# One hybrid attention, SSD and expert step on one Trainium2 core: SSD chunks moved in between the query and gate projections

## What is computed

```python
mod = jnp.dot(jax.nn.silu(cvec), lp['ada_w']) + lp['ada_b']        # 6 x 1024 columns
sh1, sc1, g1, sh2, sc2, g2 = jnp.split(mod[:, None, :], 6, axis=-1)
h = rmsnorm(x, lp['norm1']) * (1 + sc1) + sh1
proj = jnp.dot(h, lp['w_in'])                                      # 2064 columns
q, k, v, xbc, z, dt_raw = jnp.split(proj, SPLITS, axis=-1)
q = rmsnorm(q.reshape(b, L, N_HEADS, HEAD_DIM), lp['q_norm'])      # then rotated; k too
attn = block_attention(q, keys, vals)
xbc = jax.nn.silu(centred_dwconv(xbc, lp['conv_w'], lp['conv_b']))
ssm, h_fin = ssd_mixer(xbc, z, dt_raw, h0, ...)                    # chunks of 128, both directions, times silu(z)
x = x + g1 * jnp.dot(jnp.concatenate([attn, ssm], axis=-1), lp['w_out'])
h2 = rmsnorm(x, lp['norm2']) * (1 + sc2) + sh2
x = x + g2 * expert_choice_ffn(h2, ...)                            # 16 experts, SwiGLU
```

## Time and profile before

| | us |
|---|---|
| median of 3 runs | 2115.31 (2110.8 to 2117.49) |
| the profiled execution, its time | 2113.7 |
| its span, first to last instruction | 2112.0 |
| mean granted clock of TensorE, 1.0 being 2.4 GHz | 0.932 |
| PE busy | 1876.4 (89%) |
| DVE busy | 648.7 (31%) |
| ACT busy | 351.0 (17%) |
| POOL busy | 195.9 (9%) |

### The profile page before, as it was taken

The page is one execution under the profiler, slowest core; times in us unless marked ns, Lnnn a source line. Parts: engine busy times, 40 slices in busy tenths (PEclk is TensorE's granted clock), DMA queues, the critical chain, the costliest instruction groups (busy, mean ns, idle before and its releaser), DMA issues. The chain is left out here.

```text
span 2112.0 us, 34478 instructions
## 1 busy us (share of the span) xinstructions
PE 1876.4 (89%) x14896; PEld 909.8 (43%) x14896; DVE 648.7 (31%) x1360; ACT 351.0 (17%) x872; POOL 195.9 (9%) x265
## 2 busy tenths in 40 slices
PE   4999788984999999999839998789859999999997
PEld 1453664442344434444315536644413434444343
DVE  2314557334111212112123155673341112112121
ACT  2211533120100100001022115332101001000010
POOL 0002310000000001000010023100000001010010
PEclk9999769996999999999869997799979999999998
DMA  9632010332999999999953320103339999999993
GB/s 388 237 127 93 27 58 1 140 141 90 335 404 393 408 406 401 411 398 403 385 226 120 119 103 18 58 1 149 142 108 342 405 396 403 407 398 409 405 404 111
DMA packets 56870, 526.47 MB, mean 249 GB/s; under 512 B 11950, under 2 KB 13598, under 8 KB 26046
## 3 DMA queue, kind: packets, MB, share of 16 engines
q1 hardware_dynamic: 42062, 482.30, 56.5%
q0 software_dynamic: 6336, 21.63, 4.3%
q10 hardware_dynamic: 8416, 21.76, 2.7%
HBM read 503.91 MB, written 24.38 MB: 250 GB/s over the span
## 5 line engine op out<-in xcount | busy, mean ns | idle before, releaser
L503 PE MATMUL PS<-arena,xe 128*32 128x512 f32 x6144 | 673.4, 598 | 3.8 <-DVE xe L1212 3.8
L503 PEld LDWEIGHTS PS<-arena,xe 128*32 128x32 f32 x6144 | 195.9, 111 | 457.9 <-issue 453.6
L527 PE MATMUL PS<-arena,hdT 128*32 128x512 f32 x1536 | 269.0, 600 | 12.4 <-DMA arena<-w_exp 10.5
L529 PE MATMUL PS<-arena,hdT 128*32 128x256 f32 x1024 | 266.6, 383 | 0.0
L1223 DVE TENSOR_TENSOR RA<-RA,PS 96x512 f32<-96x512 f32 (+2 forms) x96 | 63.2, 684 | 648.8 <-ACT RA L948 646.1
L580 PE MATMUL PS<-arena,RB 128*128 128x512 f32 (+1 forms) x480 | 176.7, 528 | 0.0
L532 PE MATMUL PS<-arena,hdT 128*32 128x256 f32 x1536 | 157.3, 382 | 0.0
L533 PE MATMUL PS<-arena,hdT 128*32 128x256 f32 x512 | 153.6, 382 | 0.0
L853 PE MATMUL PS<-arena,RB 128*128 128x512 f32 x320 | 138.8, 593 | 2.0 <-DVE RB L1471 2.0
L948 ACT ACTIVATE RA<-PS 96x512 f32<-96x512 f32 x32 | 19.0, 593 | 689.4 <-PE PS L503 689.4
L580 PEld LDWEIGHTS PS<-arena,RB 128*128 128x128 f32 x480 | 90.4, 190 | 87.5 <-issue 81.3
(11 more groups left out here) (269 smaller groups left out, 1818.4 us busy)
## 6 DMA issues: line engine op xcount, KB each, us to landing
arena<-w_exp SPq DMA_DIRECT2D x192, 2048.0 KB, 12.3
arena<-ada_rest SPq DMA_DIRECT2D x16, 2048.0 KB, 7.6
arena<-w_in SPq DMA_DIRECT2D x4, 4128.0 KB, 31.3
ada<-ada_first SPq DMA_DIRECT2D x8, 2048.0 KB, 22.9
arena<-w_out SPq DMA_DIRECT2D x2, 4096.0 KB, 12.9
RC<-x_res ACTq DMA_DIRECT2D x2, 2560.0 KB, 9.8
x_res<-RC ACTq DMA_DIRECT2D x10, 512.0 KB, 2.6
normed_rows<-RA ACTq DMA_DIRECT2D x10, 512.0 KB, 2.6
```

The source lines that it names most:

```text
L503: last = mm(PS[GRP * q:GRP * (q + 1), c * 512:(c + 1) * 512], xe[:, k, GRP * grp:GRP * (grp + 1)], w[:, col_, :], start=(k == 0), stop=(k ...
L527: mm(PS[GRP * q:GRP * (q + 1), 1536:2048], tok(q), w[:, 0:512], start=first, **flags)
L529: mm(PS[96:P, 1536 + grp * REST:1536 + (grp + 1) * REST], tok(grp), w[:, MAIN:D], start=first and grp == 0, **flags)
```

## The change

- w_in is stored by groups of use: the six chunks of convolved columns (x0 and x1, three each), keys with step sizes (kv), queries (q) and z, each a transfer and a semaphore of its own. Layer 0 loads x0, x1, slabs 0 and 1, kv, q, the small loads, z, then the other slabs. Layer 1 loads x0, x1, kv and z, then waits for the rows of x and loads slabs 0 and 1 and q.
- A slab stands behind each chunk of the convolved columns (six), the last two behind key tiles 1 and 3.
- PSUM: the products use four banks up to number 16 and two from there on; the other banks serve the SSD pieces.
- `project` takes a `midway` that runs between its steps k = 3 and 4. The token transposes stand from key tile 3 to query tile 1, the sums behind query tile 1, the modulation rows amid query tile 2, `cumulated` and `scores` of chunks 0 and 1 and the state products around query tiles 2 to 4. Chunk t stands amid z tile t.
- Queries are squared, summed and rotated tile by tile inside DVE's loop over chunks (`head_sums`, `head_norms`), keys before the sums; the powers are split (`query_root`). The product with silu(z) moves from `tile_out` behind the rotation.
- Chunk buffers move into the part of the arena that the convolved columns' weights leave, temporaries into RA.

The core of the diff (indented 8 less; "..." for what is left out; removed lines only where they help):

```diff
-C_Q, C_KV, C_DT, C_XBC, C_Z = 0, 512, 768, 784, 1552
+KV_DT = 272
+W_Z, W_X, W_K, W_Q = 0, 4096, 10240, 12416
...
+EW = [a.rearrange("p (r c) -> p r c", r=2) for a in (arena[:, 8192:10240], arena[:, 10240:12288])]
...
+        def input_weights(group, a, n):
+            sp.dma_start(arena[:, a:a + n], row(w_in, l)[:, :, a:a + n].rearrange("a p n -> (a p) n")).then_inc(win_in[group].sem, 16)
+        def slab(c):
             if c >= 2:
...
+        if l:
+            sp.wait_ge(gu_used.sem, gu_used.at(l, 0))
+        input_weights("x0", W_X, 3072)
+        input_weights("x1", W_X + 3072, 3072)
+        if l:
+            input_weights("kv", W_K, KD * KV_DT)
+            input_weights("z", W_Z, KD * 512)
+            sp.wait_ge(x_in.sem, x_in.at(l, 2))
+            sp.wait_ge(dn_used.sem, dn_used.at(l, 0))
+            slab(0)
+            slab(1)
+            input_weights("q", W_Q, KD * 512)
+        else:
+            slab(0)
+            slab(1)
+            input_weights("kv", W_K, KD * KV_DT)
+            input_weights("q", W_Q, KD * 512)
+            sp.dma_start(ropes[:, :, :], rope).then_inc(rope_in, 16)
+            caches(0)
+            input_weights("z", W_Z, KD * 512)
+        for c in range(2, KD):
+            slab(c)
+        if l == 0:
+            sp.dma_start(x_res[0:CTX, :], x_prompt).then_inc(x_copied, 16)
...
+        def project(width, lhs, rhs, midway=None):
...
+        def states():
+            pe.wait_ge(tok_ev.sem, tok_ev.at(l, NT))
+            pe.wait_ge(mod_rdy2.sem, mod_rdy2.at(l, 1))
+            pe.wait_ge(gm_rdy.sem, gm_rdy.at(l, 1))
...
+            if t or r:
+                pe.wait_ge(c_rdy.sem, c_rdy.at(l, 2 * t + r))
+            else:
+                pe.wait_ge(cs_rdy.sem, cs_rdy.at(l, 1))
+                pe.wait_ge(hp_rdy.sem, hp_rdy.at(l, 1))
             for h in range(8):
...
+        for c in range(NC_):
+            if c == 0:
+                pe.wait_ge(win_in["x0"].sem, win_in["x0"].at(l, 1))
+            if c == 3:
+                pe.wait_ge(win_in["x1"].sem, win_in["x1"].at(l, 1))
+            for _, s0, sn in (SETS[1], SETS[0]):
+                project(sn, lambda k: arena[:, W_X + c * 1024 + k * P:W_X + c * 1024 + (k + 1) * P], lambda k: hT[:, k, s0:s0 + sn])
+            rest_of_modulation(c)
...
+        pe.wait_ge(win_in["kv"].sem, win_in["kv"].at(l, 1))
+        for t in range(NT):
+            project(KV_DT, tokens(t), lambda k: arena[:, W_K + k * KV_DT:W_K + (k + 1) * KV_DT])
+            if t == 1:
+                rest_of_modulation(6)
+            if t == 3:
+                rest_of_modulation(7)
+                conv_tokens(0)
+        conv_tokens(1)
+        def queries(t, midway):
+            project(512, tokens(t), lambda k: arena[:, W_Q + k * 512:W_Q + (k + 1) * 512], midway)
+        pe.wait_ge(win_in["q"].sem, win_in["q"].at(l, 1))
+        queries(0, lambda: conv_tokens(2))
+        conv_tokens(3)
+        queries(1, lambda: conv_tokens(4))
+        sums()
+        first_states()
+        queries(2, second_rows)
+        cumulated(0, 0)
+        scores(0)
+        queries(3, lambda: cumulated(0, 1))
+        states()
+        queries(4, lambda: cumulated(1, 0))
+        cumulated(1, 1)
+        scores(1)
+        pe.wait_ge(win_in["z"].sem, win_in["z"].at(l, 1))
+        for t in range(NT):
+            def chunk():
+                if t and t + 1 < NT:
+                    cumulated(t + 1, 1)
+                if t:
+                    from_states(t)
+                else:
+                    last_states()
+                within_chunk(t)
+                if t + 2 < NT:
+                    scores(t + 2)
+            project(512, tokens(t), lambda k: arena[:, W_Z + k * 512:W_Z + (k + 1) * 512], chunk)
             if t + 2 < NT:
-                scores(t + 2)
-                for r in range(2):
-                    cumulated(t + 2, r)
-            if t == 0:
-                pe.wait_ge(hf_ev.sem, hf_ev.at(l, 1))
+                cumulated(t + 2, 0)
         pe.wait_ge(y_done.sem, y_done.at(l, NT))
...
+        def clamped(t, r):
+            act.wait_ge(seg_ps.sem, seg_ps.at(l, 2 * t + r + 1))
+            if t >= 2:
+                act.wait_ge(yd_ps.sem, yd_ps.at(l, 2 * (t - 2) + r + 1))
+            for h in range(8):
+                o = 1024 + h * P
+                last = A(EW[t % 2][:, r, h * P:(h + 1) * P], PS[:, o:o + P], ACT.Relu, scale=-1.0, bias=cs[:, r, t, h:h + 1])
+            last.then_inc(c_rdy.sem, 1)
+        def decays(t):
+            for r in range(2):
+                act.wait_ge(c_rdy.sem, c_rdy.at(l, 2 * t + r + 1))
+                A(EW[t % 2][:, r, :], EW[t % 2][:, r, :], ACT.Exp, scale=-1.0).then_inc(e_rdy.sem, 1)
+        keys_evac(0)
+        keys_evac(1)
+        keys_evac(2)
         conv_silu(NC_ - 1)
...
+        keys_evac(3)
+        tokens_evac(0)
+        keys_evac(4)
         A(negA[:, :], bp[:, B_AL:B_AL + 16], ACT.Exp)
+        tokens_evac(1)
         act.wait_ge(dt_abs.sem, dt_abs.at(l, 1))
         A(dte[:, :, :], dts[:, :, :], ACT.Exp, scale=-1.0).then_inc(dt_e.sem, 1)
...
         act.wait_ge(rows0_2.sem, rows0_2.at(l, 1))
         act.wait_ge(ada2_used.sem, ada2_used.at(l, KD))
         for q in (0, 1):
             last = A(mrows2[32 * q:32 * q + 2, :, :], PS[32 * q:32 * q + 2, 3072:4096].rearrange("p (b c) -> p b c", b=2), ACT.Copy)
         last.then_inc(rows_act2.sem, 1)
...
+        tokens_evac(2)
+        queries_evac(0)
+        tokens_evac(3)
+        tokens_evac(4)
+        queries_evac(1)
+        act.wait_ge(cs_rdy.sem, cs_rdy.at(l, 1))
+        A(wend[:, :, :, :], wend[:, :, :, :], ACT.Exp)
+        A(ecs[:, :, :, :], cs[:, 0:2, :, :], ACT.Exp)
+        A(etot[:, :, :, :], cs[:, 2:4, :, :], ACT.Exp).then_inc(cs_e.sem, 1)
+        queries_evac(2)
+        clamped(0, 0)
+        clamped(0, 1)
+        decays(0)
+        queries_evac(3)
         act.wait_ge(S_ps.sem, S_ps.at(l, 4))
+        clamped(1, 0)
+        queries_evac(4)
+        clamped(1, 1)
+        decays(1)
         for t in range(NT):
...
             if t == 0:
                 act.wait_ge(hf_ps.sem, hf_ps.at(l, 1))
                 act.wait_ge(h0_ps.sem, h0_ps.at(l, 1))
                 A(hst[:, :, :, :].rearrange("p r m c -> p (r m c)"), bank(6), ACT.Copy).then_inc(hf_ev.sem, 1)
...
+            elif t + 1 < NT:
+                clamped(t + 1, 1)
+                decays(t + 1)
+            act.wait_ge(ip_ps.sem, ip_ps.at(l, n + 1))
+            A(z_t[:, t, :], bank(place(n)), ACT.Silu).then_inc(ip_ev.sem, 1)
+            n += 1
+            if t + 2 < NT:
+                clamped(t + 2, 0)
+            if t:
+                act.wait_ge(y_done.sem, y_done.at(l, t))
+                squares(l, 1, t - 1, cat[:, t - 1, 512:1024], sqtmp)
+        act.wait_ge(y_done.sem, y_done.at(l, NT))
+        squares(l, 1, NT - 1, cat[:, NT - 1, 512:1024], sqtmp)
         act.wait_ge(hf_ev.sem, hf_ev.at(l, 1))
         for r in range(2):
...
-        link(V.tensor_copy(cs[:, :, :, :].rearrange("p a t h -> p (a t h)"), PS[:, 0:160]))
+        link(V.tensor_copy(cs[:, :, :, :].rearrange("p a t h -> p (a t h)"), PS[:, 1024:1184]))
         V.tensor_tensor(wend[:, :, :, :], cs[:, 2:4, :, :], cs[:, 0:2, :, :], ALU.subtract).then_inc(cs_rdy.sem, 1)
+        dve.wait_ge(h0_ps.sem, h0_ps.at(l, 1))
+        dve.wait_ge(tok_ps.sem, tok_ps.at(l, NT))
+        also(hp_rdy, V.tensor_copy(hprev[:, 0, :, :].rearrange("p r c -> p (r c)"), bank(3)), l, 1)
...
         for g in range(2):
             rows = slice(g * HD, (g + 1) * HD)
             for s in range(1, 4):
...
+        masked(1)
         for t in range(NT):
             tile_out(t)
             if t + 2 < NT:
-                weights(t + 2)
+                masked(t + 2)
+            if t + 1 < NT:
+                weights(t + 1)
+            head_norms(t)
+            dve.wait_ge(ip_ev.sem, ip_ev.at(l, 23 + t))
+            y = cat[:, t, 512:1024]
+            V.tensor_tensor(y, y, z_t[:, t, :], ALU.mult).then_inc(y_done.sem, 1)
+            if t + 1 < NT:
+                head_sums(t + 1)
         for t in range(NT):
             mean_eps(l, 1, t, 512)
...
+        pool.wait_ge(rows0_2.sem, rows0_2.at(l, 1))
+        TT(ksq, kv_t[:, :, 0:P], kv_t[:, :, 0:P], ALU.mult).then_inc(ks_rdy.sem, 1)
+        pool.wait_ge(ku_rdy.sem, ku_rdy.at(l, 1))
+        TT(hs[:, :, 8:10], hs[:, :, 8:10], mhalf[:, 0:10].rearrange("p (t h) -> p t h", h=2), ALU.pow).then_inc(kr_rdy.sem, 1)
+        def query_squares(t):
             pool.wait_ge(ip_ev.sem, ip_ev.at(l, 18 + t))
-            TT(RA[:, t * 512:(t + 1) * 512], q_t[:, t, :], q_t[:, t, :], ALU.mult).then_inc(qs_rdy.sem, 1)
-        TT(RA[:, 2560:3200].rearrange("p (t c) -> p t c", t=NT), kv_t[:, :, 0:P], kv_t[:, :, 0:P], ALU.mult).then_inc(qs_rdy.sem, 1)
-        pool.wait_ge(hsu_rdy.sem, hsu_rdy.at(l, 1))
-        TT(hs[:, :, :].rearrange("p t h -> p (t h)"), hs[:, :, :].rearrange("p t h -> p (t h)"), mhalf[:, :], ALU.pow).then_inc(hrs_rdy.sem, 1)
```

(73 more changed lines are left out.)

382 lines of the change are left out of this document (147 added, 235 removed).

## The result

The changed kernel takes 2032.49 us (median of 4 runs, 2024.5 to 2034.4), the kernel before 2113.74 (4 runs): ratio 0.9607, 95% interval 0.9577 to 0.9638. Forecast were 2036 us in 2022 to 2074. The profiled execution took 2032.23 us, its span is 2030.5; 2034.1 had been worked out for it.

What follows compares the result with a forecast made beforehand. PE, busy 89%, was taken to lose time where it idles or runs at its lower clock. Gains of 61.6, 7.9 and 10.1 (79.6) from 2113.7 gave 2034.1, plus 1.6 for the median: 2036 us, range 2022 to 2074.

Steps and rivals of the forecast that it cites:

- Part 1, the mechanism: SSD stage: nearly all its work runs beside half projections at full clock; gain 30.8 us a layer, bounds 12 and 34.
- Part 1, the slacks: Hand-overs beside the half projections: no other engine ends last; clamping slack 1 us, VectorE 11.8 us of a 14.8 us chunk.
- two meetings at 1.6 us each: Chunk loop: VectorE's work meets GpSimd's twice a chunk, bringing VectorE to 15.0 us, level with PE.
- Part 2: Layer 0's start: loading weights by use, x0 and x1 first, removes the first projection's stall; gain 7.9 us.
- Part 3: Between the layers: slabs queued behind x speed up the last scatter and x load; gain 10.1 us (7 to 13).
- Attention, output projection, routing and experts keep their order.: Stages behind the SSD work: order stays, and routing hides the first expert slab, which leaves with the last z product.
- The swinging clock: Rival, chance 0.20: PE's clock falls once a chunk at 2.4 to 4 us, 12 to 20 a layer; 2060 to 2076.
- one wait of a microsecond or two is enough: Chunk loop, argument for the swinging-clock rival: one such wait in a chunk makes the clock fall.
- they don't raise it: SSD stage: its products keep a clock but don't raise it, read from 273 to 289, busy 15.93 of 16 at 0.51.
- VectorE as the bound: Rival, chance 0.10: in the chunk loop each microsecond above PE's period costs 4 a layer; at 3 above, 2060.
- the clock stays low in the woven part: Rival, chance 0.05: from the queries on some 115 us of work a layer would double; in full 2266 us.
- More gain: Rival, chance 0.03: attention starts at the high clock, 4 us less a layer, 2028 or below.

Runs made afterwards that it cites:

- experiment 1: Changed kernel with all query and z products first and all SSD pieces behind them; 2115.39 us, ratio 1.0017 to the kernel before.
- experiment 2: Changed kernel with only the loop over the five chunks moved behind the last z product; 2084.71 us, ratio 0.9871 to the kernel before.
- experiment 8: Changed kernel with the four products of each query tile's rotation done twice on VectorE; 2031.98 us, ratio 0.9629 to the kernel before.
- experiment 9: Changed kernel with the four products of each query tile's rotation done four times in all on VectorE; 2058.33 us, ratio 0.9752 to the kernel before.
- experiment 10: Changed kernel with ScalarE's ten DMA issues of states, keys and values moved from ahead of the attention into the chunk loop; 2018.66 us, ratio 0.9563.

## Why the prediction was right

**Part 1, the mechanism.** Right. The SSD work of a layer fits between half projections at the high clock, with no wait inside; experiments 1 and 2 take the halves away and both the idle time and the low clock return. The gain is 34.7 us a layer, not 30.8, so the term is mis-sized by 3.9; it lies above the upper bound of 34 too. About 2 us are the changes between groups: I took 2 and they cost nothing, for the next group starts before the row above ends. By the same overlap the SSD pieces fill 203.4 - 155.4 - 1.7 = 46.3 us and not 48.3. The bound "no cost of changes" was the true value. The tail was 1.7 (forecast 1.6), the state products 3.7 (3.6).

**Part 1, the slacks.** The clamping's slack of 1 us was 1.2. VectorE's 11.8 a chunk was right in work (12.3 to 12.6 of 14.5, meetings with GpSimd included), and its slack larger than the period shows, since it may fall behind over several chunks. The count of two meetings at 1.6 us each was too high. The Trainium skill (GPSIMD Engine Reference, "1. Specifications") says that GpSimd shares its SBUF interfaces with VectorE and contends with VectorE's instructions that have two SBUF inputs. The trace agrees, at 1.44 against 0.69 us and no loss with one operand in PSUM, and experiment 8 too: with VectorE shifted against GpSimd's products the weights took 3.56 us instead of 2.62.

**Part 2.** Right in the result: the first projection is unbroken, and layer 0's stretch shrinks by 42.5, 7.8 more than layer 1's (7.9 forecast). The reason I gave was too narrow: the two groups need not be first. Slab 2 cost nothing: z was issued at 59.8, as forecast.

**Part 3.** 10.1 forecast, 11.3 in the traces, 12.2 when it was undone. The scatter took 7.15 (7.5 forecast), x 8.94 (10.4 with its issue), though the load that this price came from had met hardly any other traffic (295.4 to 305.2, a DMA share of 0.77); why x came sooner stays open. Of the two gains 0.5 went back at the transposes of layer 1, at a lower clock.

**"Attention, output projection, routing and experts keep their order."** The order is kept, but the time is not, and this is the step that failed. The other terms were 8.9 us too low in sum (7.7 in part 1, 1.2 in part 3, part 2 as forecast); 7.0 of them were given back behind the key transposes, 1.8 in layer 0 and 5.2 in layer 1. So the forecast is 1.9 us off because two errors cancel, which is luck.

Of the 7.0, 1.3 and 1.2 us go at the start of attention. ACT's ten issues stood there before too, but took 4.7 us, from 290.49 to 295.2, and were over with the transposes, which ran at the low clock in part (until 295.09). Now the transposes are done 3.1 us after their start and the issues take 6.0, so PE waits for them. The first expert slab leaves with the last z product. That used to be a stage earlier; now it is at 246.34, and its transfer meets the issues. Windows of the changed kernel and of the kernel before during the issues, then window and issues of experiment 9, where VectorE's work holds the attention back until the slab, which left at 256.17, is in:

```profile
248.00:254.00 6.00, 3.05 (x26) 2.81 (x26) 2.22 (x8) 0.70 (x2) 2.63 (x5) 1.00 0.89 339
290.50:295.50 5.00, 4.58 (x26) 4.34 (x26) 2.33 (x8) 0.95 (x3) 2.61 (x5) 0.68 0.28 65
...
266.50:271.30 4.80, 4.74 (x22) 4.74 (x23) 2.39 (x9) 0.72 (x2) 2.63 (x5) 0.50 0.25 55
267.43 2.88 ACTq L1176 DMA_DIRECT2D new_h<-hst  x6
270.34 0.44 ACTq L1178 DMA_DIRECT2D new_k<-RD  x1
```

In all six such places (both layers of experiments 1, 2 and 9) the slab has left 10 us or more before, the share is 0.25 or 0.26 and the issues take 4.7 us, in the same place and order as in the changed kernel. So it is the traffic that slows them, and not PE's clock, which was 1.00 in experiment 10 while they took 4.7 too. That the wait hangs on the issues is shown by experiment 10. A further 0.7 goes in layer 1, where the sixteen score products took 2.08 us behind the long wait and 1.16 in the kernel before, and 0.5 behind the output projection of layer 0. The rest, 3.3 us, lies behind the output projection of layer 1, where the code is the same and the fourteen traces differ by as much; I take it for the clock's scatter and not for an effect of the change, but no run separates the two.

**The rivals.** The swinging clock exists and costs 6.5 us each time, more than my 2.4 to 4. It did not come, because the loop has no wait at all; "one wait of a microsecond or two is enough" was wrong for 0.66 and 1.57 us between half projections. Where the small products stand alone it is nearer to the truth: in experiment 2 the clock fell behind a wait of 2.26 us in layer 0, and behind three such waits in layer 1 it did not. And "they don't raise it" holds for the stretch that I read it from, but not always: in experiment 1, layer 1, the clock rose between the product from the state before (2.08 us, low) and within_chunk (3.84, high), with no large product near. The Trainium skill (TensorE: Matmul & The Clock Gate, "A second HAM failure mode: psum-queue depth-cycling") warns that short idle spells while PE goes through its PSUM banks make the clock swing. The traces agree for waits of 2.42 and 2.48 us in the chunk loop, and not for all of those. VectorE as the bound did not come; with its work 3.2 us a chunk above PE's period PE waited in the fifth chunk only, and there the clock came down too. That the clock stays low in the woven part fell at once: 1.00 from the first projection to the key transposes. "More gain" did not come either, for the scores started at the low clock behind the wait; with the issues out of the way (experiment 10) they start at the high one, and from key transposes to scores it takes 3.8 us instead of the 6.6 of the kernel before.

## What to carry to other kernels

When small matmuls with hand-overs leave the tensor engine idle and at half clock, put them between halves of large ones that are ready anyway; price the result as the sum of start-to-start times, without a charge for changing, and check the tightest hand-over. Moving work away from in front of a stage uncovers what the stage's end had hidden: list the DMA issues that stand in the queue of the engine that the next stage waits for, and put them where that engine idles. Behind a serial point, the loads that others want at once go first in the DMA queue, and what is wanted later waits for them.

## What the runs showed of the hardware

- Between half projections PE's clock outlived twelve waits of 0.66 and 1.57 us, and fell after two of six waits of 2.48 and after both of 2.42 that began 1.1 us after one of 0.27. In a loop of small products alone it fell after a wait of 2.26 in one layer and outlived three of 2.26 in the other. After a wait of 4.83 sixteen small products took 2.08 us, after one of 0.74 they took 1.16.
- A DVE addition of two SBUF operands, 128x512, took 1.44 us where it met a POOL product and 0.69 alone, and one of a PSUM and an SBUF operand 0.69 beside such a product; four weight products took 2.50 alone, 2.62 and 3.56 by how much of POOL's work they met.
- ACT's issues of new_k and new_v took 0.92 and 0.94 us at a DMA share of 0.89, and 0.44 and 0.45 at 0.24 to 0.28, in the chunk loop and ahead of the attention alike.
